# Gate and up chunks 1 to 9 with three seven-product units, and three low halves a chunk by adding transfers

## The reference

```python
D_MODEL = 2048
SEQ = 256
D_FF = 5632

def _swiglu_ffn(x, norm_g, w_gate, w_up, w_down):
    h = _rmsnorm(x, norm_g)
    return (jax.nn.silu(h @ w_gate) * (h @ w_up)) @ w_down
...
h = h + 0.5 * _swiglu_ffn(h, ffn1_norm[l], ffn1_w_gate[l], ffn1_w_up[l], ffn1_w_down[l])
...
h = h + 0.5 * _swiglu_ffn(h, ffn2_norm[l], ffn2_w_gate[l], ffn2_w_up[l], ffn2_w_down[l])
```

## Time and profile before

| | us |
|---|---|
| runs, median of 3 | 2593.36 |
| runs, lowest and highest | 2592.0, 2594.75 |
| profiled execution: span from first to last instruction | 2591.4 |
| TensorE busy in the span | 2562.1 (99%) |
| VectorE busy | 1954.8 (75%) |
| ScalarE busy | 1339.8 (52%) |
| GpSimd busy | 189.2 (7%) |

### The profile page before, as it was taken

How to read it: one execution, slowest core, us unless ns; L and a number is a source line. 1 busy time by engine, 2 the same in 40 slices (tenths; PEclk the granted TensorE clock), 3 DMA queues, 4 the chain that set the end, 5 groups by cost and what they waited for, 6 DMA issues and landing times.

```text
span 2591.4 us, 34224 instructions
## 1 busy us (share of the span) xinstructions
PE 2562.1 (99%) x13659; PEld 2103.4 (81%) x13659; DVE 1954.8 (75%) x2311; ACT 1339.8 (52%) x1568; POOL 189.2 (7%) x346
## 2 busy tenths in 40 slices
PE   8999999999999999999999999999999999999998
PEld 7888888888888777878788888888888888888887
DVE  6888888887767796959666766555668888888876
ACT  5555555555556366446455544433455455555554
POOL 2000000000000011010001112000100000000000
PEclk9999999999999999999999999999999999999999
DMA  6767676667776575656488779643767677766655
GB/s 213 232 210 242 210 236 218 217 208 228 216 210 195 184 228 159 179 165 181 146 280 257 252 245 281 201 155 130 239 190 230 222 226 225 227 219 218 210 201 175
DMA packets 278576, 548.21 MB, mean 212 GB/s; under 512 B 25020, under 2 KB 35424, under 8 KB 278032
## 3 DMA queue, kind: packets, MB, share of 16 engines
q1 hardware_dynamic: 253904, 478.60, 58.3%
q0 software_dynamic: 24192, 66.89, 8.8%
q10 hardware_dynamic: 320, 0.53, 0.1%
HBM read 508.15 MB, written 37.77 MB: 211 GB/s over the span
## 4 chain that ended last, share of the span: by engine, by line
PE 86%; DVE 8%; ACT 3%; DMA 2%; issue 1%; POOL 0%; SPq 0%; DVEq 0%; ACTq 0%; POOLq 0%
PE pp L794 14%; PE pp L795 14%; PE pp L796 14%; PE pp L415 11%; PE pp L416 11%; PE pp L417 11%; DVE wlo L376 2%; PE pa L794 1%; PE pb L796 1%; PE pb L795 1%; PE pb L794 1%; PE pa L795 1%; PE pa L796 1%; ACT whi L371 1%; DMA raw<-in_ffn_w_up 1%
## 5 line engine op out<-in xcount | busy, mean ns | idle before, releaser
L376 DVE TENSOR_TENSOR wlo<-raw,whi 128x1024 fp32r<-128x1024 f32 (+1 forms) x764 | 919.6, 1216 | 345.9 <-ACT whi L371 326.2
L371 ACT ACTIVATE whi<-raw 128x1024 fp32r<-128x1024 f32 (+1 forms) x764 | 798.0, 1053 | 626.5 <-PE pp L417 438.1
L794 PE MATMUL pp<-whi,xhi 128*128 128x512 f32 x1040 | 404.6, 389 | 0.0
L795 PE MATMUL pp<-whi,xlo 128*128 128x512 f32 x1040 | 404.6, 389 | 0.0
L796 PE MATMUL pp<-wlo,xhi 128*128 128x512 f32 x1040 | 404.6, 389 | 0.0
L415 PE MATMUL pp<-whi,xhi 128*128 128x512 f32 (+1 forms) x928 | 370.6, 399 | 0.7 <-DVE xlo L533 0.7
L417 PE MATMUL pp<-wlo,xhi 128*128 128x512 f32 (+1 forms) x928 | 359.6, 388 | 0.1
L416 PE MATMUL pp<-whi,xlo 128*128 128x512 f32 (+1 forms) x928 | 359.6, 387 | 0.0
L847 ACT ACTIVATE whi<-tw 128x1024 fp32r<-128x1024 f32 x124 | 131.6, 1062 | 276.3 <-PE pp L796 131.6
L794 PEld LDWEIGHTS pp<-whi,xhi 128*128 128x128 f32 x1040 | 195.2, 188 | 40.7
L796 PEld LDWEIGHTS pp<-wlo,xhi 128*128 128x128 f32 x1040 | 195.2, 188 | 40.6
(11 more groups left out here) (528 smaller groups left out, 3669.7 us busy)
## 6 DMA issues: line engine op xcount, KB each, us to landing
raw<-in_ffn_w_gate SPq DMA_DIRECT2D x176, 512.0 KB, 4.3
raw<-in_ffn_w_up SPq DMA_DIRECT2D x176, 512.0 KB, 4.7
raw<-in_ffn_w_down SPq DMA_DIRECT2D x176, 512.0 KB, 4.6
raw<-in_w_in SPq DMA_DIRECT2D x144, 512.0 KB, 4.3
hid_dram<-hid_t POOLq DMA_DIRECT2D x43, 512.0 KB, 5.0
xq<-hid_dram POOLq DMA_DIRECT2D x156, 128.0 KB, 3.8
raw<-in_w_lift SPq DMA_DIRECT2D x32, 512.0 KB, 5.9
raw<-in_w_out SPq DMA_DIRECT2D x32, 512.0 KB, 5.1
```

Of the source, the lines that this page charges most:

```text
L371: nc.scalar.activation(whi[:, s, :, 0:width], raw[:, r % RING, :, 0:width], ACT.Copy).then_inc(whi_ready, 1)
L376: nc.vector.tensor_tensor(wlo[:, s, :, 0:width], raw[:, r % RING, :, 0:width], whi[:, s, :, 0:width].bitcast(F32), ALU.subtract).then_inc( ...
L794: nc.tensor.matmul(out, a_hi, whi[:, s, block, :], start=start, stop=False)
L795: nc.tensor.matmul(out, a_lo, whi[:, s, block, :], start=False, stop=False)
```

## The change

Chunks 1 to 9 of both FFNs (`THREE`) get a third unit, row group 5, and units stand behind plain slots 1, 3 and 5 (`gu_units`). A pair then has ten plain slots, five of gate and five of up, and three units; chunk 10 keeps its two. The activations' combinations for group 5 are made in chunk 0 (`xs_5`, `xshi_5`, `xslo_5`).

In these chunks the low halves of plain slots 0, 2 and 4 (`LO_ADDED`) are no longer VectorE's. ScalarE writes minus the rounded weights into a buffer of its own (`less_hi`, two buffers `alo` in turn), GpSimd issues a transfer that adds the raw weights onto it (`add_raw`), and TensorE reads the low half there. The raw buffer of such a slot comes free when the adding transfer has landed (`wait_lo`). ScalarE's negated copy for slot 0 stands behind the previous chunk's last plain slot, those for slots 2 and 4 between the second and the third copy of the unit ahead of them.

The work around the units moves: the combining goes to plain slots 8 and 9, the split of the hidden part to plain slots 8 (ScalarE) and 9 (VectorE), and the silu of a chunk behind the first copy of the next one. GpSimd issues two adds ahead of the store of the hidden part and one behind it.

```diff
+THREE = range(1, NFC - 1)
+def gu_units(i):
+
+    return ((5, 6, 7), (1, 3, 5)) if i in THREE else ((6, 7), (1, 5))
...
+LO_ADDED = (0, 2, 4)
...
+        alo = [at(f"alo{k}", kib, [SK, CW], F32R) for k, kib in enumerate((AR + 32, AR + 76))]
...
+        def wait_lo(eng, n):
+
+            if n in ADDED:
+                eng.wait_ge(whi_ready, n + 1)
+                eng.wait_ge(sem(f"lo_added{ADDED[n] % 2}"), 16 * (ADDED[n] // 2 + 1))
+            else:
+                eng.wait_ge(wlo_ready, n + 1 - sum(a < n for a in ADDED))
+
         def raw_free(sp, r):
             if r >= RING:
-                sp.wait_ge(wlo_ready, freed_by[r - RING] + 1)
+                wait_lo(sp, freed_by[r - RING])
...
+        def less_hi(act, n):
+
+            r, k = raw_of[n], ADDED[n]
+            act.wait_ge(*loaded(r))
+            if k > 1:
+                act.wait_ge(slot_used, list(ADDED)[k - 2] + 1)
+            nc.scalar.activation(alo[k % 2][:, :, :], raw[:, r % RING, :, :], ACT.Copy, scale=-1.0).then_inc(sem("lo_less_hi"), 1)
+
+        def add_raw(pool, n):
+
+            k = ADDED[n]
+            pool.wait_ge(sem("lo_less_hi"), k + 1)
+            nc.gpsimd.dma_start(alo[k % 2][:, :, :].bitcast(F32), raw[:, raw_of[n] % RING, :, :],
+                                accum_op=ALU.add).then_inc(sem(f"lo_added{k % 2}"), 16)
...
             for i in range(NFC):
-                hidden_out(pool, tag, i)
+                added = [prods[tag + "gu"][2 * i + 2]["pair"]["plain"][t][2] for t in LO_ADDED] if i + 1 in THREE else []
+                for n in added[:2]:
+                    add_raw(pool, n)
+                hidden_out(pool, tag, i, lambda: [add_raw(pool, n) for n in added[2:]])
...
             hi(w + 1, whi[:, (w + 1) % RING, :, :], tw[:, 0:2, :])
+            if ahead is not None:
+                ahead()
...
+                    if t == 0 and i - 1 in THREE:
+                        gate_silu(i - 1)
+                    if t in after:
+                        n = after.index(t)
+                        ahead = (lambda: less_hi(act, added[n + 1])) if n + 1 < len(added) else None
+                        unit_act(act, pair, n, (tag, "gu", i), ahead)
+                    if t == after[-1] + 1:
                         act.wait_ge(nat_ready, n0 + i)
                         copy_first(act, pair, cb[:, 0, :])
-                    if t == pair["na"] + 3:
+                    if t == after[-1] + (3 if i in THREE else 4):
...
+                if i + 1 in THREE:
+                    less_hi(act, gu[2 * i + 2]["pair"]["plain"][LO_ADDED[0]][2])
...
                 for t, (_, _, w, _) in enumerate(pair["plain"]):
-                    split_lo(dve, w, 0)
+                    if w not in ADDED:
+                        split_lo(dve, w, 0)
...
-                    if t == pair["na"] + 2:
+                    if t == after[-1] + 3:
                         combine(dve, pair, cb, (tag, "gu", i))
-                    if t == pair["na"] + 3:
+                    if t == after[-1] + 4:
                         combine_last(dve, cb, (tag, "gu", i))
                         v.tensor_tensor(cb[:, 0:2, :], pair_of(gate), cb[:, 0:2, :], ALU.add).then_inc(sem(gate["released"][0]), 1)
+                        if i in THREE:
+                            hidden_lo(dve, tag, i - 1, hhi[:, 4 * i - 4:4 * i, :], hlo[:, 4 * i - 4:4 * i, :])
```

More of the change, by code:

```diff
@@ L233, in count_marks @@
     for tag in ("f1", "f2"):
-        sums.append((tag, "x"))
-        acts.append((tag, "x"))
-        banks.append((tag, "x"))
+        for marks in (sums, acts, banks):
+            marks += [(tag, "x"), (tag, "x5")]
         for i in SEVEN:
-            for u in GU_UNITS:
+            for u in gu_units(i)[0]:
                 sums += [(tag, "gu", i, u, step) for step in (1, 2, 3)]
@@ L253, in count_marks, with added_slots @@
     return [{name: n + 1 for n, name in enumerate(marks)} for marks in (sums, acts, banks)]
+def added_slots(prods):
+    return [prods[tag + "gu"][2 * i]["pair"]["plain"][t][2] for tag in ("f1", "f2") for i in THREE for t in LO_ADDED]
 def build(nc, A):
     prods, turns, nats, moved, raw_of, freed_by = plan()
+    ADDED = {n: k for k, n in enumerate(added_slots(prods))}
     SUMS, ACTS, BANKS = count_marks()
@@ L668, in turn_out @@
             nc.gpsimd.dma_start(scratch, hid_t[:, :, :, :].rearrange("p b m j -> p (b m j)")).then_inc(sem("hid_stored"), 16)
+            if between is not None:
+                between()
             pool.wait_ge(sem("hid_stored"), 16 * d + 16)
@@ L795, in product @@
             nc.tensor.matmul(out, a_lo, whi[:, s, block, :], start=False, stop=False)
-            return nc.tensor.matmul(out, a_hi, wlo[:, s, block, :], start=False, stop=stop)
+            return nc.tensor.matmul(out, a_hi, (wlo[:, s, :, :] if lo is None else lo)[:, block, :], start=False, stop=stop)
         def plain_pe(pe, pair, t, acts, tts=range(TT), used=1):
@@ L966, in ffn_act, with gate_silu @@
                     forms_hi(act, xs_gu[:, :, :, :], xshi[:, :, :, :], (tag, "x"))
+                    forms_hi(act, xs_5[:, :, :], xshi_5[:, :, :], (tag, "x5"))
+            less_hi(act, gu[2]["pair"]["plain"][LO_ADDED[0]][2])
+            def gate_silu(i):
+                gate = gu[2 * i]
+                act.wait_ge(sem(gate["released"][0]), gate["released"][1])
+                for tt in range(TT):
+                    op = nc.scalar.activation(gs[:, tt, :], cb[:, tt, :], ACT.Silu, scale=rstd[:, tt:tt + 1])
+                op.then_inc(sem("acts_ready"), 1)
@@ L967, in ffn_act @@
             for i in SEVEN:
                 pair = gu[2 * i]["pair"]
-                gate = pair["a"]
+                after = pair["after"]
+                added = [pair["plain"][t][2] for t in LO_ADDED] if i in THREE else []
                 for t, (_, _, w, _) in enumerate(pair["plain"]):
                     split_hi(act, w, 0)
-                    if t in GU_AFTER:
-                        unit_act(act, pair, GU_AFTER.index(t), (tag, "gu", i))
-                    if t == pair["na"]:
+                    if t == 0 and i - 1 in THREE:
[5 more added lines that the diff above has]
+                    if t == after[-1] + 1:
@@ L975, in ffn_act @@
                         act.wait_ge(nat_ready, n0 + i)
                         copy_first(act, pair, cb[:, 0, :])
-                    if t == pair["na"] + 3:
+                    if t == after[-1] + (3 if i in THREE else 4):
+                        if i == NFC - 1:
+                            act.wait_ge(slot_used, pair["units"][-1][1] + UW)
                         hidden_hi(act, tag, i - 1, hhi[:, 4 * i - 4:4 * i, :])
-                    if t == pair["na"] + 4:
-                        act.wait_ge(sem(gate["released"][0]), gate["released"][1])
-                        for tt in range(TT):
-                            op = nc.scalar.activation(gs[:, tt, :], cb[:, tt, :], ACT.Silu, scale=rstd[:, tt:tt + 1])
-                        op.then_inc(sem("acts_ready"), 1)
+                    if t == after[-1] + 5:
+                        gate_silu(i)
@@ L1055, in ffn_dve @@
                     forms(dve, xf, xs_gu, (tag, "x"))
+                if j == 5:
+                    link(dve, v.tensor_tensor(whole_5[:, :, :], xhi[:, 10:12, :].bitcast(F32), xlo[:, 10:12, :].bitcast(F32), ALU.add))
+                    forms(dve, whole_5, xs_5[:, :, :].unsqueeze(1), (tag, "x5"))
             forms_lo(dve, xs_gu[:, :, :, :], xshi[:, :, :, :], xslo[:, :, :, :], (tag, "x"))
+            forms_lo(dve, xs_5[:, :, :], xshi_5[:, :, :], xslo_5[:, :, :], (tag, "x5"))
             for i in SEVEN:
@@ L2946, in _ @@
         def _(pe):
-            pe.wait_ge(ident_ready, 1)
+            pe.wait_ge(consts_ready, 1)
             gain_turn(pe)
```

86 lines of the change are left out of this document (46 added, 40 removed).

## The result

| | before | after |
|---|---|---|
| median of the runs, us | 2594.06 (4 runs, 2592.0 to 2595.4) | 2749.33 (4 runs, 2743.04 to 2750.0) |
| ratio, 95% interval | | 1.059 (1.0575 to 1.0605) |
| span of the profiled execution, us | 2591.4 | 2741.3 |

The account below looks back on a forecast made before the run. TensorE's matmuls bound the old kernel; the change saves 12.2 us there, but a closed path of VectorE and loads sums to 44.73 us a chunk against 41.48: +40 us, 2634 us, range 2610 to 2660 (8 in 10: 2588 to 2700).

Parts of the forecast that it names:

- link 4: Second unit's third low half to third unit's first sum: 6.24 us, of which 1.0 for transfers beside the loads.
- the edge: First chunks of each FFN: VectorE starts 2.9 us ahead, so chunk 1 takes 41.5 us and chunk 2 43.5.
- Link 7: Plain slot 8's low half to the next chunk's first sum, through combining, last sums and silu: 9.69 us.
- Links 1 to 3, 5 and 6: Path's three units, the reload before unit 2, the way to plain slot 8: 7.88, 5.24, 5.29, 5.29, 5.1 us.
- the bare path: VectorE's closed path through a chunk without the 1.0 us for transfers beside the third unit's loads: 43.73 us.
- X: Time of one adding transfer from issue to landing, taken as 6.1 us.
- the adds' chain: Load, copy and add in turn through raw buffer 0: 42.7 us a chunk, ruling if an add exceeds 6.8.
- B: Rival: the path closes within TensorE's 41.48 us a chunk, all the saving arrives, 2581 us; chance 0.16.
- C: Rival: the path comes to 42.2 us a chunk, a draw at 2588 to 2599 us; chance 0.06.
- A: Rival: adding transfers land in over 6.8 us and set the chunk; 2695 us at 8; chance 0.28.

Follow-up runs that it names:

- e1: The changed kernel, but GpSimd issues the hidden part's loads only once the third unit's up half has landed; 2670.04 us, ratio 1.0268.
- e5: The changed kernel without adding transfers (VectorE makes those low halves) and with the hidden part's loads held until the third unit's up half landed; 2624.43 us, ratio 1.0114.
- e3: The changed kernel without adding transfers or negated copies, VectorE making all low halves; 2652.18 us, ratio 1.0199.
- e2: The changed kernel with its three adding transfers per chunk made plain copies of the same bytes; 2672.34 us, ratio 1.0278.

## Why the prediction was wrong, and what of it held

**The step that failed is link 4's +1.0** for the add and the hidden part's loads beside the third unit's, with bounds of 0 and 2. In the chunk read above it was 11.4 - 5.24 = 6.2, over the upper bound by 4.2. It came from a row with one load beside one store (5.3 against 3.8), and that row has neither of the two things that met here. Alone each is about what was taken: +1.2 on units 2 to 3 for the adds (e1 over e5), +1.6 for the hidden loads (e3 over e5). Together they are +5.7. The square of e1, e3, e5 and the change shows this; what makes the two together worse than their sum inside the transfer engines it does not show. The five rows from 182 to 192 us have a mean share of 1.0 at 247 GB/s, the first of them 137, against 225 at a share of 0.71 in the old chunk: busy time per byte had risen by nearly 30%, the bytes by 10%. The Trainium skill's page "DMA: Bandwidth & Descriptors", section "Queues, rings and completion order", says that each transfer engine serves its queues in turn, a packet at a time; by that a load shares each engine with whatever the other queue holds. The landings of 8.0 and 10.9 agree with it, but no run here shows the turns themselves.

The account for one FFN, nine chunks, first sums: predicted 41.5 + 43.5 + 7 x 44.73 = 398.1, measured 459.0 in the first. Units 2 to 3 make 9 x (16.36 - 11.53) = 43.5 of the 61, units 1 to 2 6.3, units 3 to next 6.8. The rest is the edge: chunks 1 and 2 were given 41.5 and 43.5 and took 51.0 and 51.3, as VectorE's lead at the start does nothing against late loads. In the second FFN it is 451.9, 54 more than predicted. 2634 + 61 + 54 = 2749, the measured median. (Chunk 10, to which the prediction gave 1.6 us for being entered late, lost nothing in the first FFN: from its first sum to the first down matmul it takes 43.1 us, before 43.3. That is 3 us off the sum for both.)

**Link 7** is 0.75 longer on the mean. In e2, e3 and e5, which have no adding transfer, this part takes 20.0 to 20.1 as predicted, and with two or three adds 20.6 to 20.8. In the chunk shown its wait is for the next unit's up half, 1.27 us. That half was issued at 206.63, 0.8 behind the next chunk's first add, and landed after 6.2 us; the prediction's sum for this link had no load in it. In e1, without the collision at unit 3, the part is as long.

**What held.** The sign, and the mechanism: a path of VectorE and loads that passes no TensorE work. Links 1 to 3, 5 and 6 are within 0.13 us in the chunk read, and the bare path's three parts within 0.15 (e5). That VectorE's and ScalarE's sums don't bind: 36.5 and 26.7 us busy in the 51.2 of that chunk. The wait ahead of unit 2 of 2 us or less (0.50, and at most 2.0 in the first FFN) and more ahead of unit 3 (7.75). X: a median of 5.3 us in the change, predicted 6.1, under the 6.8 from which the adds' chain was to rule; and it doesn't rule in the change. What the prediction cited against the change also stands: with plain copies of the same bytes instead of adds the engines are held 1.4 us instead of 3.1. The Trainium skill's "Collectives: The Full Stack", section "The bandwidth ceiling: the fold count and why AG ≠ RS ≠ AR", says of a ring collective that its reducing transfer reads two sources and moves at about half a copy's rate; the measured 3.1 to 1.4 us, a factor of 2.2, agrees. In the prediction that rule was set against X alone, where it did no harm. It belonged to link 4, as time that a *neighbour* loses: leaving out `accum_op` alone took 4.4 us off the chunk (e2, 46.62 against 51.00).

**The rivals.** B (the path closes, 2581) is out: with neither adds nor hidden loads beside it, it is 43.99. C, a draw, fell with B. A was right about the danger and wrong about the place in the change itself: TensorE waits 5.5 us for adds from 100 to 480 us, and 34.5 for low halves of units. Of those, 29.6 us in seven waits stand ahead of unit 3's first slot (such as the 4.52 at 194.40 below), so where TensorE would wait was wrong too: not mostly at second to fourth slots.

## What to carry to other kernels

Price a transfer twice: what its own reader waits, and what it takes from the transfers issued within its landing time. For the second, list by start times everything that all queues have in flight at the moment where a path has no slack; a price from a row with one neighbour doesn't carry over to two. And before an engine's work is taken off it, ask whether the path has that engine's sum in it, or a buffer's round trip: here VectorE had 15 us to spare in a chunk of 51 and was still on the path.

## What the runs showed of the hardware

- **An adding transfer** of 512 KB within the core's memory lands in 5.1 us against 3.0 for a copy of the same bytes, and takes the 16 transfer engines 3.1 us against 1.4 (e1, e2).
- **Two kinds of transfer beside the loads cost more here than the sum of each**: units 2 to 3 take +1.2 us with the adds and +1.6 with the hidden part's loads, +5.7 with both (e5, e1, e3, the change).
- **TensorE's clock** fell in the changed kernel. In TensorE's timeline the last matmul ahead of the third unit starts at 189.49; the next starts at 194.40, and after it matmuls stand 0.43 apart:

```profile
189.49 0.39 PE L846 MATMUL pp<-wlo,xhi 128*128 128x512 f32 x1
194.40 0.80 PE L844 MATMUL pa<-whi,xhi 128*128 128x512 f32 x1 [4.52 <-DVE wlo L918]
...
195.42 0.63 PE L846 MATMUL pa<-wlo,xhi 128*128 128x512 f32 x1
195.84 0.63 PE L844 MATMUL pp<-whi,xhi 128*128 128x512 f32 x1
```

The stretch from 194 to 196 us stands at a granted clock of 0.50, the lower level of 1.2 GHz, after a wait of 4.5 us; before, it was 1.00 throughout the chunk. It costs little here: links 5 to 7 follow at 5.3, 5.0 and 11.06, and e1, whose mean granted clock is 0.999 against 0.985, takes 20.73 from unit 3 to the next against 20.83. No run shows what such a wait costs where TensorE is the bound.
